# Expert tokens packed by an indirect DMA of token rows and 8 transposes, and the spreading of results in two parts

## The reference, cut to what matters

```
g_idx = argmax(hf @ w_rg + b_rg)                     # one of 4 expert groups
e_prob = softmax(logits of the 4 experts in it)
top_p, top_i = top_k(e_prob, 2)                      # 2 experts of the 4
weight = g_prob * top_p / sum(top_p)
for e in range(16):                                  # EXPERT_FF = 512
    a = silu(hf @ w_gate[e]) * (hf @ w_up[e])
    y = y + gates[:, e:e+1] * (a @ w_down[e])
```

## Time and profile before

| | us |
|---|---|
| timed executions, median of 3 | 1602.88 |
| lowest, highest | 1602.78, 1604.02 |
| span of the profiled execution | 1606.5 |
| in it: TensorE busy | 1538.3 |
| VectorE busy | 539.9 |
| ScalarE busy | 292.8 |
| GpSimd busy | 27.9 |

### The profile page before, as it was taken

One profiled execution on the slowest core, in us unless ns is written; L12 is line 12 of the kernel. 1 busy time (PEld: TensorE's weight loads), 2 busy tenths in 40 slices (PEclk: granted clock), 3 DMA queues, 4 the chain that ended last, 5 costly groups with the idle time before them and its releaser, 6 DMA issues.

```text
span 1606.5 us, 20275 instructions
## 1 busy us (share of the span) xinstructions
PE 1538.3 (96%) x8656; PEld 983.4 (61%) x8656; DVE 539.9 (34%) x1110; ACT 292.8 (18%) x616; POOL 27.9 (2%) x56
## 2 busy tenths in 40 slices
PE   7999899899999999999999998998999999999997
PEld 5777668577766644445367776685776675444543
DVE  3313654561132411211233165636411423121122
ACT  2013321140121201001100142212311212100102
POOL 0000000000000000000000000000000000000000
PEclk9999999999999999999999999989999999999999
DMA  7233323784267599999723242329733757999991
GB/s 311 105 117 146 137 91 123 297 335 163 105 256 300 206 420 398 399 406 412 290 72 138 105 159 96 132 106 345 310 130 137 302 217 310 405 401 404 411 395 62
DMA packets 31262, 387.77 MB, mean 241 GB/s; under 512 B 3776, under 2 KB 4224, under 8 KB 6592
## 3 DMA queue, kind: packets, MB, share of 16 engines
q1 hardware_dynamic: 26048, 357.74, 56.5%
q0 software_dynamic: 5120, 28.69, 4.5%
HBM read 361.66 MB, written 24.75 MB: 241 GB/s over the span
## 4 chain that ended last, share of the span: by engine, by line
PE 90%; DMA 3%; DVE 3%; ACT 1%; DVEq 1%; issue 1%; ACTq 0%; SPq 0%
PE psum L565 37%; PE psum L1147 14%; PE psum L925 9%; PE psum L1167 7%; PE psum L1192 4%; PE psum L1122 4%; DMA ring<-stream 2%; PE psum L581 1%; DMA work<-acum_flat 1%; PE psum L572 1%; PE psum L1133 1%; PE psum L959 1%; PE psum L1004 1%; PE psum L1022 1%; PE psum L975 1%
## 5 line engine op out<-in xcount | busy, mean ns | idle before, releaser
L565 PE MATMUL psum<-h,ring 128*128 128x320 f32 x1664 | 459.0, 436 | 0.9 <-issue 0.9
L565 PEld LDWEIGHTS psum<-h,ring 128*128 128x128 f32 x1664 | 315.6, 191 | 136.2 <-issue 9.7
L1147 PE MATMUL psum<-ring,work 128*64 128x512 f32 x768 | 170.3, 592 | 1.4 <-ACT work L1539 1.4
L565 PE MATMUL psum<-mem,ring 128*128 128x256 f32 x512 | 124.5, 400 | 7.1 <-DMA ring<-stream 7.1
L1147 PEld LDWEIGHTS psum<-ring,work 128*64 128x64 f32 x768 | 55.0, 137 | 110.2 <-issue 108.5
L565 PEld LDWEIGHTS psum<-mem,ring 128*128 128x128 f32 x512 | 100.6, 200 | 29.4 <-DMA ring<-stream 7.9
L1167 PE MATMUL psum<-work 128*64 128x512 f32 x512 | 113.4, 595 | 0.7 <-ACT work L1550 0.7
L925 PE MATMUL psum<-work,ring 128*128 128x320 f32 x384 | 104.9, 433 | 0.9 <-ACT work L1314 0.9
L925 PEld LDWEIGHTS psum<-work,ring 128*128 128x128 f32 x384 | 72.3, 190 | 30.9 <-ACT work L1314 1.8
L565 PE MATMUL psum<-work,ring 128*128 128x320 f32 x256 | 72.2, 444 | 11.7 <-DMA ring<-stream 10.5
L2078 DVE TENSOR_TENSOR x<-x,psum 128x320 f32<-128x320 f32 x128 | 62.4, 488 | 54.9 <-PE psum L1192 49.2
(11 more groups left out here) (299 smaller groups left out, 1382.2 us busy)
## 6 DMA issues: line engine op xcount, KB each, us to landing
ring<-stream SPq DMA_DIRECT2D x111, 2048.0 KB, 11.0
work<-stream SPq DMA_DIRECT2D x32, 2048.0 KB, 10.1
states_out<-stream SPq DMA_DIRECT2D x24, 2048.0 KB, 9.9
st_out<-states_out POOLq DMA_DIRECT2D x12, 1024.0 KB, 11.4
st_out<-work POOLq DMA_DIRECT2D x6, 1024.0 KB, 7.4
work<-acum_flat POOLq DMA_DIRECT2D x10, 256.0 KB, 3.9
k_mem<-acum_flat POOLq DMA_DIRECT2D x10, 256.0 KB, 3.6
ring<-stream SPq DMA_DIRECT2D x4, 512.0 KB, 9.1
```

Of the source, the lines that this page charges most:

```text
L565: mm = pe.matmul(out, w[:, a:a + P], rhs[:, j, :], start=(j == 0), stop=(j == KD - 1))
L1147: mm = pe.matmul(psum[ab * CAP:(ab + 1) * CAP, up, :], h_packed[:, p % 2, k, ab * CAP:(ab + 1) * CAP], w[:, a:a + BANK], start=(k == 0), s ...
```

## The change

For pairs 1 to 7 the packing by products is replaced. The turned tokens `h_tok` are written once per layer to a DRAM scratch `h_rows` by GpSimd, four DMAs. For each pair VectorE works out the number of the token in each slot, from the turned `picked`: where it is over 0 the token's number counts, and the sum over tokens plus 512 is the row; an empty slot gets row 512, which is out of bounds and not fetched. GpSimd gathers the rows with an indirect DMA into one of two buffers `slot_rows` (which lie where h_tok was), slots on partitions. TensorE then turns the 128 x 1024 block by 8 transposes (`unpack`) into banks 4 and 5, where ScalarE's copy finds it as before. Pair 0 is packed as before.

For this, `picked` of a pair is made and turned two pairs ahead (`turn_picked`), into one of four buffers `picked_ts`. The spreading of a pair's result is split: five products after gate_up m = 0 of the next pair, the other three after its gate_up m = 3. The order of the PSUM banks of the spreads changes, and hidden's transposes go to bank 7 in place of 6. A table `token` of 320 columns is added to the constants.

```diff
+        h_rows = [nc.dram_tensor(f"h_rows{l}", (T, D), F32, kind="Internal").ap() for l in range(DEPTH)]
-        picked_t = view(work, 8960, T)
+        slot_rows = [view(work, 3072, D), view(work, 4096, D)]
+        picked_ts = [view(work, at, T) for at in (8960, 5120, 5440, 5760)]
+        token_of = view(work, 11328, T)
-        SPREAD = [2, 3, 6, 7]
+        SPREAD = [2, 3, 6, 7, 2, 3, 6, 2]
+        IN_FIRST = 5
 # TensorE
+                def unpack(p):
+                    n_p = L * PAIRS + p
+                    pe.wait_ge(s_gathered[p % 2], 16 * gathers(L, p))
+                    pe.wait_ge(s_packout, 2 * n_p)
+                    for half in range(2):
+                        for i in range(4):
+                            j = 4 * half + i
+                            mm = pe.transpose(psum[:, 4 + half, i * P:(i + 1) * P],
+                                              slot_rows[p % 2][:, j * P:(j + 1) * P], ident)
+                        mm.then_inc(s_pack, 1)
+                def turn_picked(p):
+                    n_p = L * PAIRS + p
+                    pe.wait_ge(s_picked, n_p + 1)
+                    if p >= 3:
+                        pe.wait_ge(s_added, (n_p - 2) * KD - 1)
+                    elif p == 2:
+                        pe.wait_ge(s_ctout, n_p)
+                    transposes([(psum[:, 7 if p == 0 else 6, t * P:(t + 1) * P], picked[:, p % 2, t, :])
+                                for t in range(3)]).then_inc(s_ct, 1)
 # in spread
-                            pe.wait_ge(s_ctout, n_p + 1)
+                            pe.wait_ge(s_ctout, L * PAIRS + min(p + 2, PAIRS - 1) + 1)
-                            pe.wait_ge(s_added, n_p * KD + j - 3)
+                            pe.wait_ge(s_added, n_p * KD + (5 if j == 7 else j - 3))
 # before and in the loop over the pairs
                 pack_prompt(0)
                 pack_sample(0)
+                turn_picked(0)
+                turn_picked(1)
...
                         if m == 0 and p > 0:
-                            spread(p - 1, range(KD))
-                        if m == 3 and p + 1 < PAIRS:
-                            pack_prompt(p + 1)
+                            spread(p - 1, range(IN_FIRST))
+                    if p > 0:
+                        spread(p - 1, range(IN_FIRST, KD))
                     pe.wait_ge(s_hid, n_p + 1)
                     if p > 0:
-                        pe.wait_ge(s_added, n_p * KD)
+                        pe.wait_ge(s_added, (n_p - 1) * KD + 4)
+                    else:
+                        pe.wait_ge(s_ctout, n_p + 1)
...
                     if p + 1 < PAIRS:
-                        pack_sample(p + 1)
-                    pe.wait_ge(s_picked, n_p + 1)
-                    transposes([(psum[:, 7, t * P:(t + 1) * P], picked[:, p % 2, t, :])
-                                for t in range(3)]).then_inc(s_ct, 1)
+                        unpack(p + 1)
+                    if p + 2 < PAIRS:
+                        turn_picked(p + 2)
                     pe.wait_ge(s_hidtout, n_p + 1)
                     if p > 0:
+                        pe.wait_ge(s_added, n_p * KD)
 # VectorE
+                def rows_of_slots(p):
+                    n_p = L * PAIRS + p
+                    src = psum[:, 7 if p == 0 else 6, 0:T]
+                    dve.wait_ge(s_ct, n_p + 1)
+                    if p == 1:
+                        dve.wait_ge(s_rows, 64 * (L + 1))
+                        dve.wait_ge(s_pack, 2 * n_p)
+                    if p > 0:
+                        dve.scalar_tensor_tensor(out=token_of, in0=src, scalar=0.0, in1=k_("token", T),
+                                                 op0=ALU.is_gt, op1=ALU.mult, accum_out=row_sum[:, p:p + 1])
+                        dve.drain()
+                        dve.tensor_scalar(row_of[:, p:p + 1], row_sum[:, p:p + 1], float(NO_ROW), None, ALU.add)\
+                            .then_inc(s_row_of, 1)
+                    dve.tensor_copy(picked_ts[p % 4], src).then_inc(s_ctout, 1)
...
+                rows_of_slots(0)
+                rows_of_slots(1)
                 for p in range(PAIRS):
                     n_p = L * PAIRS + p
+                    if p + 2 < PAIRS:
+                        pick(p + 2)
                     if p > 0:
-                        added(p - 1)
+                        added(p - 1, range(IN_FIRST))
                     dve.wait_ge(s_gu, n_p + 1)
                     dve.wait_ge(s_sg, n_p + 1)
                     dve.tensor_tensor(hidden, hidden, psum[:, 1, :], ALU.mult).then_inc(s_hid, 1)
-                    if p + 1 < PAIRS:
-                        pick(p + 1)
-                    dve.wait_ge(s_ct, n_p + 1)
-                    dve.tensor_copy(picked_t, psum[:, 7, 0:T]).then_inc(s_ctout, 1)
+                    if p > 0:
+                        added(p - 1, range(IN_FIRST, KD))
+                    if p + 2 < PAIRS:
+                        rows_of_slots(p + 2)
 # GpSimd, per layer, behind the stores of the memory projection
+                for t in range(2):
+                    pool.wait_ge(s_htout, L * 6 + 4 + t)
+                    pool.dma_start(h_rows[L][tok(t), :], h_tok[:, t, :]).then_inc(s_rows, 16)
+                pool.wait_ge(s_htout, L * 6 + 6)
+                for half in range(2):
+                    f = slice(half * BANK, (half + 1) * BANK)
+                    pool.dma_start(h_rows[L][tok(2), f], h_tok[rows_in(2, half), 2, f]).then_inc(s_rows, 16)
+                pool.wait_ge(s_rows, 64 * (L + 1))
+                for p in range(1, PAIRS):
+                    n_p = L * PAIRS + p
+                    pool.wait_ge(s_row_of, L * (PAIRS - 1) + p)
+                    pool.wait_ge(s_pack, 2 * n_p - 2 if p > 1 else 2 * n_p)
+                    pool.indirect_dma_start(slot_rows[p % 2], None, h_rows[L],
+                                            bass.IndirectOffsetOnAxis(ap=row_of[:, p:p + 1], axis=0),
+                                            bounds_check=T - 1, oob_is_err=False).then_inc(s_gathered[p % 2], 16)
```

More of the change, by code:

```diff
@@ L45 @@
 PAIRS = E // 2
+NO_ROW = 512
 ROPE_BASE = 10000.0
@@ L106 @@
           ("decay", RH * P), ("decay_s", RH * LG), ("qdecay", RH * P), ("qdecay_s", RH * DS),
-          ("kend", RH), ("kend_s", RH), ("restart", T), ("rank", EPG * EPG), ("slots", CAP), ("fold", EG + E)]
+          ("kend", RH), ("kend_s", RH), ("restart", T), ("rank", EPG * EPG), ("slots", CAP), ("fold", EG + E),
+          ("token", T)]
 CAT, CN = layout_of(CONSTS)
@@ L155, in constants @@
     put("slots", np.tile(np.arange(1, CAP + 1.0)[None], (P, 1)))
+    put("token", np.tile(np.arange(T)[None] - float(NO_ROW), (P, 1)))
     return c.astype(np.float32)
@@ L191, in build @@
         spilt = ctx.enter_context(nc.sbuf_tensor("spilt", [P, DEPTH], mybir.dt.int32))
+        row_of = ctx.enter_context(nc.sbuf_tensor("row_of", [P, PAIRS], mybir.dt.uint32))
+        row_sum = sb("row_sum", PAIRS)
         psum = ctx.enter_context(nc.psum_tensor("psum", [P, 8, BANK], F32))
@@ L390, in build @@
         s_picked = sem("s_picked")
+        s_rows = sem("s_rows")
+        s_row_of = sem("s_row_of")
+        s_gathered = [sem(f"s_gathered{i}") for i in range(2)]
         s_pack = sem("s_pack")
@@ L436, in sum_bank, with gathers @@
             return 0 if k == 1 or L == DEPTH else 7
-        SPREAD = [2, 3, 6, 7]
+        SPREAD = [2, 3, 6, 7, 2, 3, 6, 2]
+        IN_FIRST = 5
+        def gathers(L, p):
+            return L * (PAIRS // 2 - (p % 2 == 0)) + (p + 1) // 2
         def tok(t):
@@ L1190, in spread @@
                         if j >= 4:
-                            pe.wait_ge(s_added, n_p * KD + j - 3)
-                        pe.matmul(psum[:, SPREAD[j % 4], 0:T], y_pair[:, j * P:(j + 1) * P], picked_t,
+                            pe.wait_ge(s_added, n_p * KD + (5 if j == 7 else j - 3))
+                        pe.matmul(psum[:, SPREAD[j], 0:T], y_pair[:, j * P:(j + 1) * P], picked_ts[p % 4],
                                   start=True, stop=True).then_inc(s_spread, 1)
@@ L1208, in moe @@
                         if m == 0 and p > 0:
-                            spread(p - 1, range(KD))
-                        if m == 3 and p + 1 < PAIRS:
-                            pack_prompt(p + 1)
+                            spread(p - 1, range(IN_FIRST))
+                    if p > 0:
+                        spread(p - 1, range(IN_FIRST, KD))
                     pe.wait_ge(s_hid, n_p + 1)
                     if p > 0:
-                        pe.wait_ge(s_added, n_p * KD)
-                    first(transposes([(psum[:, 6, 0:P], hidden[:, 0:P])]))
-                    transposes([(psum[:, 6, f * P:(f + 1) * P], hidden[:, f * P:(f + 1) * P])
+                        pe.wait_ge(s_added, (n_p - 1) * KD + 4)
+                    else:
+                        pe.wait_ge(s_ctout, n_p + 1)
+                    first(transposes([(psum[:, 7, 0:P], hidden[:, 0:P])]))
```

(28 more changed lines are left out.)

## The result

The changed kernel takes 1566.2 us (median of 4, 1564.8 to 1568.4) against 1602.8 before: a ratio of 0.978, 95% interval 0.976 to 0.979, so 36.6 us less. The forecast was 1572, with 1560 to 1597 as its range.

The account below looks back on a forecast made before the run. TensorE was taken to bound the expert stage, with the quad stream close behind and the bound after the change. From 1602.9 us, 15.8 (layer 0) and 14.7 (layer 1) were taken off: 1572 us, range 1560 to 1597.

Parts of the forecast that it names:

- The bound before: Expert stage: TensorE last, 31.20 of 31.20 us busy per pair, with the stream at 29.1 us a pair close behind.
- The change on TensorE: Expert pairs: packing dropped, 8 transposes added; period 27.05 us, 4.1 less; 28.5 us a layer if TensorE stayed the bound.
- What is late next: Expert stage: the quad stream becomes the bound at 4.95 us a quad; 14.3 us of unused buffering can be taken.
- The gathers: Expert stage: seven a layer, each adding 1.1 us to the stream, between 0.83 and 1.32.
- The sum: Expert stages: layer 0's down ends at 780.5 against 796.3, saving 15.8 us; layer 1 saves 14.7.
- The writes of h: Before the expert stage: 1.3 MB to DRAM fits the gap from 552.80 to 560.40, charged nothing; uncovered 3.3 us a layer.
- The first gather: Start of expert stage: lands near 565 to 568, wanted at 570.0; a delay up to 3 us costs nothing.
- (a): Rival, expert stage: TensorE stays the bound at 27.05 us a pair, total 1546 us; chance 3%.
- (b): Rival, stream: each gather packet costs its engine a full turn, 4.9 us a gather, total 1624 us; chance 9%.
- (c): Rival, TensorE: short waits lower its clock; a quarter of work at 1.2 GHz gives about 1607 us; chance 5%.
- (d): Rival, every pair: gathers land late because descriptor making takes GpSimd over 25 us, total some 1600 us; chance 5%.
- What would show it: Signs: quads every 4.9 to 5.1 us, ring<-stream waits in pairs 2 to 7, late periods of 30.5 to 31.5 us.

Follow-up runs that it names:

- e2: The kernel before the change, with the fourth gate_up quad (one quad in six) not loaded in pairs 1 to 7: 1602.7 us.
- e1: The changed kernel, with the fourth gate_up quad (one quad in six) not loaded in pairs 1 to 7: 1548.4 us.
- e6: The changed kernel with only the gathers of pairs 1 and 2 issued; pairs 3 to 7 turn rows that lie in the buffers: 1553.9 us.
- e3: The changed kernel with its 8 transposes of gathered rows done twice: 1566.5 us.
- e4: The changed kernel with its 8 transposes of gathered rows done four times: 1586.2 us.
- e8: The changed kernel with a seventh slot for one quad per layer, in the memory of mem and k_mem: 1569.0 us.
- e5: The changed kernel with empty slots given the last token's row, so that every gather fetches all 128 rows: 1574.9 us.
- e7: The changed kernel with the spreading not split, all eight products after gate_up m = 0: 1568.0 us.
- e9: The changed kernel with a seventh slot for one quad per layer and pair 1 packed by products as before the change: 1561.1 us.

## Why the prediction was right

- **The bound before.** "TensorE is last, but a pair also takes 6 quads": e2 shows it, 242.1 us with and without one quad in six.
- **The change on TensorE.** A period of 27.05 was forecast, 27.24 measured; the spreads are 0.2 us slower for being split (2.89 + 1.81 against 4.50). No bank wait appeared. That TensorE alone would save 28.5 us per layer is confirmed by e1: 242.1 - 214.2 = 27.9.
- **What is late next.** The stream, as forecast. Its pace was mis-sized a little: I took 4.95 us a quad as the mean of 4.85 and 5.05. The window from tenth to last quad is 191.6 us for 38 quads and six gathers, where 38 x 4.95 + 7.7 = 195.8 was forecast. With the queue never empty the rate is 427 to 428 GB/s, 4.9 us a quad. The 415 GB/s of the earlier trace rows was no measure of a deeper queue, and the trace before had one: 428 GB/s from 560.60 to 578.50, after four quads had been issued within 11 us.
- **The start of the stage.** The tenth quad was left where it lay, 27.0 us behind the start of the stage (581.2 - 554.2). It landed 28.9 us behind it (580.4 - 551.5). Its slot is freed by the first instruction of TensorE after gate_up of pair 0. Before, that was a product of packing; now it is the first transpose of hidden, which stands behind the open wait of pair 0. So the quad was issued 15.8 us after the start in place of 14.4, and took 13.1 us to land in place of 12.6. The sum has no term for this.
- **The gathers.** 1.1 us each forecast, 1.0 measured in e6; the reason given for it, the slowest engine, is not shown. "Lands about 6 us after its start" was wrong: gathers took 10.6 to 11.8 us. It cost nothing, since from pair 2 on they are issued a whole period ahead.
- **The sum.** 780.5 - 554.2 = 226.3 us for the stage of layer 0 was forecast, 224.5 measured; 227.4 and 224.4 in layer 1. Together 4.8 of the 5.8 us between 1572 and 1566.2; the other stages make up the rest. That the miss is so small is in part luck: in layer 0 the stream's stretch was 4.2 us shorter than forecast, the start 1.9 us longer, and from the last landing to the end of down it took 4.0 us in place of 3.5.
- **The writes of h.** They went earlier than forecast: issued from 541.0 us on, beside the last queued quads, and landed by 554.7. VectorE waited 0.4 us for them and TensorE not at all, so the charge of nothing holds.
- **The first gather.** Landing near 565 to 568 was forecast; it was issued at 556.37 and took 11.1, so 567.5, just when TensorE reached it. The margin that was forecast, 568 against 570.0, was not there. "A delay up to 3 us costs nothing" is not borne out: e3 and e4 lost more than the 0.5 and 0.8 us that they waited, as the transposes behind the wait ran at a lower clock, and e8 paid about 3 us for a delay of 3.7.
- **Rivals.** (a) needs 465 GB/s; e1, with a lighter stream, shows that its price was right (1548.4 against 1546), and the full stream never came near that rate. (b) is excluded by e5 and e6. (c) the clock of the changed kernel was 1.00 from 557.0 to 772.0 us; it fell to 0.50 in e8 after a wait of 3.7 us, and to 0.68 and 0.81 for some microseconds in layer 1 of e4 and e7. Two numbers of (c) don't stand. The 1607 doesn't follow from periods of 33.8: from the 1546 of (a), 12 pairs of 6.8 us more give 1627. And the 14% compares the paces of one pair and leaves out that the stage's sum decides: e4, with 18.3 us more in a stage of 224.5, 8%, had already lost 8 us a layer. (d) did not occur: a gather keeps GpSimd for 1.0 us, not 25, and TensorE does not wait for rows in the changed kernel.
- **What would show it.** Waits for ring<-stream before gate_up and down were forecast from pair 2 on. They came only before gate_up, and from pair 5 on (the first of 1.14 us, at 686.18, after 0.15 in pair 4): a period of 27.24 takes only 6 x 4.9 + 1.0 - 27.24 = 3.2 us from the stock of buffered quads. The late periods are 32.0 and 29.4 us (700.96 to 732.93 to 762.29), 30.7 in the mean, as forecast. The two parts of the spreads take 4.70 us in place of 4.50, within the 0.3 that was allowed.

## What to carry to other kernels

When two resources are both at 99%, find which one is last by taking load off the other: e2 settled what no share could. Before cutting the work of the bound engine, work out the period of the next one and the stock of buffers between them; the gain is the stock plus what the paces differ by over the stage, and not the work removed (17.7 of 28 us per layer here). Once a load stream is the bound, its foreign traffic counts in full, and a small transfer with a deadline suffers from the depth of the queue in front of it: one more quad there made the writes of h up to 5 us slower in e8 and e9. Look also at which instruction frees a buffer; removing the work that stood in front can free it later, as in pair 0 here.

## What the runs showed of the hardware

With about two quads in flight (9.7 to 12.0 us from issue to landing, medians of the kernel before) the stream made 403 GB/s at a DMA share of 0.98; with four or more (21.6 to 22.1 us) it made 427 at 1.01. The kernel before shows both rates, over the whole stage and in its first part, when four quads had just been issued:

```profile
560.60:778.50 217.90, 217.90 (x1169) 104.79 (x1167) 43.70 (x84) 20.14 (x35) 0.00 (x0) 1.00 0.98 403
560.60:578.50 17.90, 17.90 (x113) 9.25 (x111) 1.65 (x3) 2.28 (x4) 0.00 (x0) 1.00 1.00 428
```

A gather of 128 slots, 0.33 MB with 80 of them filled, needs 10.6 to 11.8 us from issue to landing beside a full stream, though its packets take only some 0.8 us of each engine (2.4% of 240 us, for seven). The four writes of h, 1.3 MB in all, took 11.3 to 11.7 us each in layer 0 of the changed kernel, and 12 to 17 us in e8. The indirect DMA of 128 rows keeps GpSimd busy for 1.0 us, as its line in the changed kernel says (ns, min/median/max, and landing in us):

```profile
L2288 POOL DMA_INDIRECT work<-h_rows,row_of x14: 988/991/1058, 556.4 to 1482.4; - x14
...
DMA to landing us min/median/max: 10.6/11.1/11.8
```

TensorE's granted clock fell behind some waits, not behind others. It fell in e8 to 0.50 (1.2 GHz of 2.4) from 568.7 to 572.9 us, after 3.7 us of waiting for the rows, where eight transposes took 1.97 us in place of 0.87. In the changed kernel waits of 1.0 to 2.5 us for quads from pair 5 on left it at 1.00.
